# A hybrid encoder layer with grouped experts: a one-hot slot table, raw rows with factors for each slot, and bounded row transfers

## What is computed

```python
def hier_moe(a, w_group_router, b_group_router, w_expert_router, b_expert_router, w_gate, w_up, w_down):
    # a is RMSNorm(h) * g_ffn_norm; 4 groups of 8 experts, 32 in all
    gp = softmax(x @ w_group_router + b_group_router)
    g_val, g_idx = lax.top_k(gp, 1)
    el = (x @ w_expert_router + b_expert_router).reshape(T, N_GROUPS, EXPERTS_PER_GROUP)
    ep = softmax(el of the chosen group)
    e_val, e_idx = lax.top_k(ep, TOP_K)          # two experts a token
    gate = g_val * e_val / sum(e_val)
    for e in range(N_EXPERTS):
        hdn = silu(x @ w_gate[e]) * (x @ w_up[e])   # 1024 -> 256
        y = y + combine[:, e:e + 1] * (hdn @ w_down[e])   # 256 -> 1024
```

## Time and profile before

| | us |
|---|---|
| median of 3 runs | 645.04 (644.75 to 645.97) |
| the profiled execution | 643.67 |
| its span in the trace | 642.0 |
| PE busy | 530.8 (83%) |
| DVE busy | 223.6 (35%) |
| ACT busy | 147.0 (23%) |
| POOL busy | 133.2 (21%) |
| mean granted clock of PE | 0.947 of full |

### The profile page before, as it was taken

One profiled execution on the slowest core, in us unless ns is written; L12 is line 12 of the kernel. 1 busy time (PEld: TensorE's weight loads), 2 busy tenths in 40 slices (PEclk: granted clock), 3 DMA queues, 4 the chain that ended last, 5 costly groups with the idle time before them and its releaser, 6 DMA issues.

```text
span 642.0 us, 8839 instructions
## 1 busy us (share of the span) xinstructions
PE 530.8 (83%) x3092; PEld 373.3 (58%) x3093; DVE 223.6 (35%) x602; ACT 147.0 (23%) x310; POOL 133.2 (21%) x200
## 2 busy tenths in 40 slices
PE   5889999997898989999725877989788897777762
PEld 4768988884444568888624545555445564434430
DVE  4743335225959562566650211121211211111110
ACT  6734343322546221121201101010100100000000
POOL 0122232032244000034323102111201232011110
PEclk9999999999999999999856989799989999889997
DMA  8730100000620039243467999999999999999992
GB/s 333 240 142 35 32 2 1 1 0 1 236 72 27 2 137 387 100 132 133 171 227 253 405 374 388 392 367 379 388 393 390 392 392 379 403 390 392 388 363 34
DMA packets 31163, 148.81 MB, mean 232 GB/s; under 512 B 7139, under 2 KB 7798, under 8 KB 18822
## 3 DMA queue, kind: packets, MB, share of 16 engines
q1 hardware_dynamic: 25376, 128.60, 50.2%
q0 software_dynamic: 5712, 19.72, 11.7%
q10 hardware_dynamic: 38, 0.01, 0.0%
HBM read 132.48 MB, written 17.00 MB: 233 GB/s over the span
## 4 chain that ended last, share of the span: by engine, by line
DMA 45%; PE 25%; issue 10%; DVE 6%; POOL 4%; ACT 1%; POOLq 0%; SPq 0%
DMA expert_w<-in_w_down 25%; DMA expert_w<-in_w_up 19%; PE ps L476 4%; PE ps L477 4%; PE ps L481 4%; PE ps L641 3%; POOL slot_tokens L1390 2%; PE ps L582 2%; DVE p_sb L1130 2%; PE ps L596 2%; PE ps L599 1%; PE ps L628 1%; PE ps L516 1%; DMA g_rows<-token_rows,idx_now 1%; PE ps L667 1%
## 5 line engine op out<-in xcount | busy, mean ns | idle before, releaser
L767 PE MATMUL ps<-expert_w,xT 128*64 128x256 f32 x1152 | 132.2, 386 | 16.4 <-DMA expert_w<-in_w_up 6.8
L767 PEld LDWEIGHTS ps<-expert_w,xT 128*64 128x64 f32 x1152 | 97.7, 140 | 55.5 <-issue 27.8
L783 PE MATMUL ps<-expert_w,hT 128*64 128x512 f32 x288 | 76.8, 681 | 23.7 <-DMA expert_w<-in_w_down 13.2
L1432 POOL DMA_INDIRECT out<-y_sb,idx_now x18 | 28.7, 1593 | 202.6 <-DVE y_sb L1302 201.8
L783 PEld LDWEIGHTS ps<-expert_w,hT 128*64 128x64 f32 x288 | 25.5, 155 | 63.1 <-issue 60.7
L1290 DVE SCALAR_TENSOR_TENSOR hid<-s_act,gate,ps 128x256 f32<-128x256 f32 x18 | 11.9, 660 | 141.5 <-ACT s_act L968 141.5
L476 PE MATMUL ps<-w_in_hi,aT_hi 128*128 128x384 f32 (+2 forms) x120 | 43.7, 368 | 0.0
L1302 DVE COPY y_sb<-ps 128x512 f32<-128x512 f32 x18 | 12.5, 692 | 89.5 <-PE ps L783 89.5
L477 PE MATMUL ps<-w_in_lo,aT_hi 128*128 128x384 f32 (+2 forms) x120 | 40.8, 344 | 0.0
L968 ACT ACTIVATE s_act<-ps 128x256 f32<-128x256 f32 x18 | 6.9, 384 | 133.7 <-PE ps L767 133.7
L973 ACT ACTIVATE y_sb<-ps 128x512 f32<-128x512 f32 x18 | 10.8, 597 | 105.6 <-PE ps L783 105.6
(11 more groups left out here) (205 smaller groups left out, 856.5 us busy)
## 6 DMA issues: line engine op xcount, KB each, us to landing
expert_w<-in_w_gate SPq DMA_DIRECT2D x32, 1024.0 KB, 9.7
expert_w<-in_w_up SPq DMA_DIRECT2D x32, 1024.0 KB, 8.5
expert_w<-in_w_down SPq DMA_DIRECT2D x32, 1024.0 KB, 10.4
w_in_raw<-in_w_in SPq DMA_DIRECT2D x8, 608.0 KB, 10.3
w_out_raw<-in_w_out SPq DMA_DIRECT2D x8, 512.0 KB, 3.6
token_rows<-rows SPq DMA_DIRECT2D x6, 528.0 KB, 3.4
out<-h_sb SPq DMA_DIRECT2D x6, 512.0 KB, 2.9
x_sb<-in_x_prompt SPq DMA_DIRECT2D x4, 512.0 KB, 9.9
```

The lines of the kernel that those rows point to most:

```text
L767: mm = pe.matmul(ps[r, 2, g * FH:(g + 1) * FH], xT[:, q.o, k, r], w_gu(b, lane, k, g), start=(k == 0), stop=(k == KD - 1))
L783: mm = pe.matmul(ps[r, 4 + half, :], hT[:, q.o, k, r], w_dn(b, lane, k, half), start=(k == 0), stop=(k == 1))
L1432: pool.indirect_dma_start(out=out, out_offset=bass.IndirectOffsetOnAxis(ap=idx, axis=0), in_=y_sb[:, buf, :], in_offset=None, compute_op=A ...
```

## The change

The slots of a pair's first pass no longer go through DRAM. For each of a token's two experts DVE makes a row of 128 with a one at its slot (`slot_a`), ACT makes three rows of 32 with a value at its expert (`slot_b`): the token number less 768, the gate and 1/rms. PE multiplies the two and sums over all tiles (`slots`), which leaves in one bank, for each slot and expert, the token, the gate and 1/rms, zeros where there is none. The spare number is added, and that is `idx_all` and `gate_all`. The scatters stay for the second passes, and POOL itself reads their indices back.

Rows are stored and gathered as h, raw (4,096 bytes, from h_sb, issued by ACT). 1/rms goes into silu's scale and into the gate; g_ffn_norm goes into the router's weights once and into the copies of the transposed rows. The column permutation is now in the transposes, which read every eighth column. Gates of second passes come from a small table of their own by a second gather. All gathers and adds have a bound: an index over 767 moves nothing.

The small setup loads and the DRAM setup move from SP's queue to the head of POOL's, the router's weights with another layout. Pairs 1 and 2 are loaded in one go behind the last h. The out stage works in halves, with transposes, logits and routing in another order.

The diff, cut; of the loops that are wholly rewritten (PE's and DVE's over the tiles, and `slot_of`) only the new and kept lines stand:

```diff
-            small = [
-                (rope_tab[:, :, :, :].rearrange("p n t r -> p (n t r)"), a["rope"]),
-                (tok_ids[:, :], a["tokens"]),
-                (w_router[:, :, 0:EG], a["w_group_router"][0].rearrange("(p k) n -> p k n", k=KD)),
-                (w_router[:, :, EG:], a["w_expert_router"][0].rearrange("(p k) n -> p k n", k=KD)),
-            ]
+            small = [(rope_tab[:, :, :, :].rearrange("p n t r -> p (n t r)"), a["rope"])]
...
-            sp.dma_start(slot_table.rearrange("(a b) c -> a (b c)", a=P),
-                         a["slots"].rearrange("(a b) c -> a (b c)", a=P)).then_inc(setup_dram, 16)
-            sp.dma_start(table[T:T + P, :], a["zeros"]).then_inc(setup_dram, 16)
-            sp.dma_start(out[T:T + P, :], a["zeros"][:, 0:D]).then_inc(setup_dram, 16)
...
-            def store_rows(i):
-                sp.wait_ge(gates_done, i + 1)
-                sp.dma_start(table[i * P:(i + 1) * P, :], rows[:, i % 2, :]).then_inc(rows_stored, 16)
-
             for i in range(NT):
                 sp.wait_ge(h_done, 2 * (i + 1))
                 sp.dma_start(out[i * P:(i + 1) * P, :], h_sb[:, i % 2, :]).then_inc(h_stored, 16)
                 if i + 1 < NT:
                     sp.dma_start(x_res[:, :], x_dram(i + 1)).then_inc(x_res_in, 16)
-                else:
-                    load_pair(sp, 1, 1, range(3))
-                if i >= 1:
-                    store_rows(i - 1)
-            load_pair(sp, 1, 1, range(3, 4))
-            store_rows(NT - 1)
-            sp.wait_ge(slots_stored, 2 * NT * 16)
+            load_pair(sp, 1, 1)
+            load_pair(sp, 2, 2)
             sp.wait_ge(counts_done, 1)
-            sp.dma_start(idx_all[:, 0:PAIRS], slot_table[0:BLOCK, :].rearrange("(s j) c -> s (j c)", j=PAIRS)).then_inc(idx_in, 16)
-            sp.dma_start(idx_more[:, :], slot_table[BLOCK:2 * BLOCK, :].rearrange("(s j) c -> s (j c)", j=PAIRS)).then_inc(idx_rest_in, 16)
-            with nc.allow_non_contiguous_dma(reason="128 indices"):
-                sp.dma_start(idx_all[:, PAIRS:], a["slots"][0:BLOCK, :].rearrange("(s j) c -> s (j c)", j=PAIRS)[:, 0:1]).then_inc(idx_rest_in, 16)
-
-            sp.wait_ge(main.gathered[0], 16)
-            load_pair(sp, 1, 1, range(4, 6))
-            load_pair(sp, 2, 2)
...
+            def slots(i):
+
+                pe.wait_ge(slot_a_done, i + 1)
+                pe.wait_ge(slot_b_done, 3 * (i + 1))
+                for c in range(2):
+                    mm = pe.matmul(ps[:, 5, 0:3 * E], slot_a[:, c, :], slot_b[:, c, :, :].rearrange("t n e -> t (n e)"), start=(i == 0 and c == 0),
+                                   stop=(i == NT - 1 and c == 1))
+                mm.then_inc(slot_mm, 1)
...
+                out_part(i, 0, False)
+                if i >= 1:
+                    h_transposes(i - 1, 1)
+                out_part(i, 0, True)
+                if i >= 1:
+                    logits(i - 1, 0)
+                    logits(i - 1, 1)
                 if i >= 2:
+                    slots(i - 2)
+                out_part(i, 1, False)
+                h_transposes(i, 0)
+                out_part(i, 1, True)
+                if i >= 1:
+                    ranks(i - 1)
+            logits(NT - 1, 0)
+            h_transposes(NT - 1, 1)
+            logits(NT - 1, 1)
+            slots(NT - 2)
             ranks(NT - 1)
+            slots(NT - 1)
...
+                blocks = src.rearrange("t (p k) -> t k p", k=KD)
                 for k in range(KD):
-                    mm = pe.transpose(ps[:, banks + k // 4, (k % 4) * P:(k % 4 + 1) * P], src[:, k * P:(k + 1) * P], ident)
+                    mm = pe.transpose(ps[:, banks + k // 4, (k % 4) * P:(k % 4 + 1) * P], blocks[:, k, :], ident)
...
+            def slot_part(i, n, col):
+
+                for c in range(2):
+                    ins = act.activation(slot_b[:, c, n, :], route_f[:, 224 + E * c:224 + E * (c + 1)], ACT.Copy,
+                                         scale=route_f[:, col(c):col(c) + 1])
+                ins.then_inc(slot_b_done, 1)
...
                 act.wait_ge(q.x_tr, n + 1)
                 bank = 0 if q is main else 6
-                act.activation(xT[:, q.o, 0:4, :], ps[:, bank, :].rearrange("p (k t) -> p k t", k=4), ACT.Copy).then_inc(q.x_act, 1)
-
-            def silu(q, n):
+                for k in range(4):
+                    ins = act.activation(xT[:, q.o, k, :], ps[:, bank, k * P:(k + 1) * P], ACT.Copy, scale=g_x[:, k:k + 1])
+                ins.then_inc(q.x_act, 1)
+
+            def silu(q, n, g):
                 act.wait_ge(q.gu_mm, n + 1)
-                act.activation(s_act[:, q.o, :], ps[:, 2, 0:FH], ACT.Silu).then_inc(q.silu_done, 1)
+                act.wait_ge(q.gate_done, (n + 1) if q is main else 3 * (n + 1))
...
-            def second_norm(i):
...
-                dve.scalar_tensor_tensor(out=rows[:, i % 2, 0:D].rearrange("t (k p) -> t p k", k=KD),
-                                         in0=h_sb[:, i % 2, :].rearrange("t (p k) -> t p k", k=KD), scalar=route_f[:, 402:403],
-                                         in1=g_ffn[:, :].rearrange("t (p k) -> t p k", k=KD), op0=ALU.mult, op1=ALU.mult).then_inc(a2_done, 1)
...
+            def slot_of(i):
                 dve.wait_ge(rank_mm, i + 1)
                 dve.wait_ge(mask_done, i + 1)
+                rank = ps[:, 6, 0:E]
+                for c in range(2):
+                    ins = dve.tensor_tensor_reduce(out=RF[:, 320 + E * c:320 + E * (c + 1)], in0=RF[:, 224 + E * c:224 + E * (c + 1)],
+                                                   in1=rank, scale=1.0, scalar=0.0, op0=ALU.mult, op1=ALU.add,
+                                                   accum_out=RF[:, 390 + c:391 + c])
+                step(ins)
+                step(dve.tensor_scalar(RF[:, 392:394], RF[:, 390:392], float(LANE), 1024.0, ALU.is_ge, ALU.mult))
+                step(dve.scalar_tensor_tensor(out=RF[:, 394:396], in0=RF[:, 390:392], scalar=RF[:, 188:189], in1=RF[:, 392:394],
+                                              op0=ALU.add, op1=ALU.add))
+                dve.tensor_scalar(RF[:, 396:398], RF[:, 394:396], -1.0, consts[:, C_TOK + i:C_TOK + i + 1],
+                                  ALU.mult, ALU.add).then_inc(val_done, 1)
+                if i >= 1:
+                    dve.wait_ge(slot_mm, i)
+                dve.tensor_scalar(slot_a[:, 0, :], iota_slot, RF[:, 394:395], None, ALU.is_equal)
+                dve.tensor_scalar(slot_a[:, 1, :], iota_slot, RF[:, 395:396], None, ALU.is_equal).then_inc(slot_a_done, 1)
...
+                residual(i, 0)
                 if i >= 1:
                     route(i - 1)
                     route_weights(i - 1)
+                residual(i, 1)
+                if i >= 1:
+                    slot_of(i - 1)
+                    table_place(i - 1)
+                    gate_row(i - 1)
...
+            dve.wait_ge(slot_mm, NT)
+            for lane in range(2):
+                r = slice(lane * LANE, (lane + 1) * LANE)
+                dve.tensor_scalar(idx_all[r, 0:PAIRS], ps[r, 5, PAIRS * lane:PAIRS * (lane + 1)], spare_row[r], None,
+                                  ALU.add).then_inc(idx_done, 1)
+            dve.tensor_copy(idx_all[:, PAIRS:], spare_row).then_inc(idx_done, 1)
+            for lane in range(2):
+                r = slice(lane * LANE, (lane + 1) * LANE)
+                dve.tensor_copy(gate_all[r, :, :].rearrange("t j n -> t n j"),
+                                ps[r, 5, E:3 * E].rearrange("t (n e) -> t n e", n=2)[:, :, PAIRS * lane:PAIRS * (lane + 1)]).then_inc(idx_done, 1)
+            gate_row(NT - 1)
...
-                dve.tensor_copy(xT[:, q.o, 4:8, :], ps[:, bank, :].rearrange("p (k t) -> p k t", k=4)).then_inc(q.x_dve, 1)
-
-            def gates(q, src, j, n, g):
+                dve.tensor_tensor(xT[:, q.o, 4:8, :], ps[:, bank, :].rearrange("p (k t) -> p k t", k=4),
+                                  g_x[:, 4:8].unsqueeze(2).to_broadcast([P, 4, P]), ALU.mult).then_inc(q.x_dve, 1)
+
+            def gates(j, g):
+
+                dve.tensor_copy(gate[:, g:g + 1, :], gate_all[:, bass.ds(j, 1), :]).then_inc(main.gate_done, 1)
+
+            def more_gates(j):
 
                 for lane in range(2):
                     r = slice(lane * LANE, (lane + 1) * LANE)
-                    dve.tensor_copy(gate[r, g:g + 1], src[r, bass.ds(j + D + PAIRS * lane, 1)]).then_inc(q.gate_done, 1)
+                    dve.tensor_copy(gate[r, 3, 0:1], more_gate[r, bass.ds(j + PAIRS * lane, 1)]).then_inc(over.gate_done, 1)
...
+            with nc.allow_non_contiguous_dma(reason="short rows"):
+                for dst, src in ((tok_ids[:, :], a["tokens"]),
+                                 (w_router[:, :, 0:EG], a["w_group_router"][0].rearrange("(k p) n -> p k n", k=KD)),
+                                 (w_router[:, :, EG:], a["w_expert_router"][0].rearrange("(k p) n -> p k n", k=KD)),
```

(54 more changed lines are left out.)

326 lines of the change are left out of this document (182 added, 144 removed).

## The result

| | before | after |
|---|---|---|
| median of the runs, us | 645.02 (644.75 to 645.97, 4 runs) | 651.0 (650.28 to 653.41, 4 runs) |
| ratio to before | | 1.0083 (95% interval 1.0051 to 1.0115) |
| the profiled execution, us (span) | 643.67 (642.0) | 650.28 (648.5) |
| mean granted clock of PE | 0.947 | 0.939 |

The prediction was 623.0, range 613 to 638, with 9% for slower. It was wrong: the kernel did not become some 3% faster but a little slower, and the interval of the ratio lies wholly above 1.

The account below looks back on a forecast made before the run. Behind 343 us DMA work was taken as the bound, with PE waiting for weights. T0 -3.6, parts in flight -1.8, rows -21 and front +1.0 gave -25.4, the build -19.7; taking -22 gave 623 us, range 613 to 638.

Parts of the forecast that it names:

- T0: SP's first weight issue for pair 3, forecast at 366.5 us, with 78 weight parts still to be issued.
- (b): DMA work behind T0: skipping empty rows of gathers and adds saves 21 us.
- The build: Sum built up from T0 at 366.5, a start of 2 and 237 us of DMA work: last part at 605.5.
- rival 2: Bound on gathers and adds saves nothing, as skipped rows still go out or take as long: about 643 us, 7%.
- unit prices: DMA costs behind 400 us: 2.51 us a weight part, 2.15 us a row transfer, a third more per byte.
- By difference, -21: Empty rows' share of the sum of differences: 21 us saved of 25.4 in all.
- (a): Stretch up to pair 3's first issue: T0 comes at 366.5, 3.6 us earlier.
- Rival 3: Second pass's rows late (T0 + 6) or the front at its upper end (+6): 632 us, 11%.
- Parts in flight, -1.8: Weights at T0: loading one and a half parts early, less the start of an empty queue, saves 1.8 us.
- Front, +1.0: Start of the kernel: setup moved from SP's to POOL's queue costs 1.0 us, between -2.7 and +6.
- rival 1: Transposes taking every eighth element load slower and PE passes the old end: 653 us at four times, 8%.
- PE below the DMA work: Whole stretch behind T0: PE ends at 592, DMA at about 604 plus 3.7, so PE has 15 us to spare.

Follow-up runs that it names:

- spread: Changed kernel with the slots of each lane of 64 in another partition order, so empty slots no longer sit side by side: 636.4 us, ratio 0.984 to before.
- after_nobound: Changed kernel without the bounds on gathers and adds, with spare rows of zeros written to both tables: 654.3 us.
- xres2: Changed kernel with two buffers for x, so that each tile's x is loaded a tile earlier: 646.6 us.
- Combined: Changed kernel with spread slots, two buffers for x, late setup transfers and weights held until the second pass's index landed: 621.6 us, ratio 0.964 to before.

## Why the prediction was wrong, step by step

- **What bounds the kernel, 78 parts behind T0**: right. 11,232 weight packets (78 times 144) follow T0 in the changed kernel, in spread and in after_nobound, and every edit that moved T0 or the rate moved the end.
- **Work behind T0, (b)**: the step that failed most, 11.5 us. The build gave 239 us, spread took 240.1 and the changed kernel 250.5. Rows were counted over all engines (a third empty) and the saving taken from the sum of the work. As work it was there: the row packets went from 61.6 us (after_nobound) to 41.8, 19.8 less where 21 was forecast. As time 5.3 came. The engines don't share the work: by the map above the fullest moves 124 of 128 rows, 3% less, where the mean is 25% less. q0's share came out as forecast and said nothing, for it is a mean over 16 engines. The prediction's rival 2 gave "takes as long" as its condition and the adds' unchanged landing as its sign; the sign was there (10.4), but it tells little, since in spread, where the bound pays, an add lands in 10.0. The prediction gave the bound either all or nothing, never a part of its worth by place.
- **A misreading in the unit prices**: a row transfer is not a third dearer per byte than weights. 58.1 us for 15.46 MB are 3.76 us a MB, against 2.39 for weights, more than half again. And the 15.46 MB are some 29 transfers, not 27, so the price was nearer 2.0 than 2.15; that puts the forecast saving 1 to 2 us too high.
- **By difference, -21**: too much even when spread evenly, where 15.7 was measured; the build's 237 plus a start of 2 came within 1.1 us of spread's 240.1. Taking the middle of the two sums put the forecast 2.3 lower than the build.
- **T0, (a)**: forecast 366.5, measured 377.0 without the front's shift (379.76 less 2.8). Last residual to landed first gather took 21.6 us, forecast 21.5 (gather issued 12.0 later, 9.6 to land): right. The other two pieces failed. The out stage grew by 5.9 and not 2.0; xres2 puts 1.4 of that on x, the rest is open. The second pass's rows were late by 3.93 and not by 1.1, and what wasn't priced is that PE's granted clock falls in that wait (0.50 from 366 to 370): products and transposes took 9.80 and 1.97 us in place of 7.13 and 1.16. The transfers themselves cost about what was said (9 to 11 each; 11.26, 5.24 and 7.10 measured). Rival 3 is this mechanism; at T0 + 6 it was mis-sized and at 11% too rare.
- **Parts in flight, -1.8**: not there. With a part and a half in flight at T0 the kernel before took 256.1 us from there, after_nobound with none 255.8. The engines were idle for 10 us ahead of T0, and holding the early pairs back brought 8 us.
- **Front, +1.0** (-2.7 to +6): +2.8 in the profile, +1.6 as the mean of eight traces (243.0 against 241.4). In size about right. What it hid is that the head of the program was the wrong place: a gain of 3.9 was to be had, and the transfers there cost 6.7 against their late place (244.22 less 237.55), 5.4 by the mean, where the cost was put at 3.9. The other fear of that paragraph, 25 us of POOL's time to write the short rows, didn't come: the seven issues took POOL from 1.46 to 6.56 us.
- **Strided stationary operand (rival 1)**: rightly held unlikely, and excluded by the trace. Loads of the block transposes, changed kernel and before:

```profile
L761 PEld LDWEIGHTS ps<-consts_sb,g_rows 128*128 128x128 f32 x128 | 16.1, 196 | 18.0 <-DMA g_rows<-token_rows,idx_all 11.3 <-issue 5.4 <-DMA g_rows<-token_rows,idx_now 1.3
```
```profile
L754 PEld LDWEIGHTS ps<-consts_sb,g_rows 128*128 128x128 f32 x128 | 14.4, 146 | 21.3 <-DMA g_rows<-token_rows,idx_now 16.3 <-issue 5.0
```

  196 ns where it was 146, 0.4 us for eight, far from the 2.0 at which it decides.
- **PE below the DMA work**: right. Combined has a weight stream that ends at 601.4, earlier than any other, and the last part is still what PE waits for. That this is near the 604 forecast is chance, for it took four more edits.
- **Tail unchanged at 15.8**: it is 18.3. The last down products took 5.37 us in place of 3.67, at a mean granted clock of 0.71 where it was 1.00: 1.7 of the 2.5. Over the twelve traces the tail lies between 15.8 and 19.1.

## What to carry to other kernels

A saving in transfers is worth mostly what it takes from the fullest DMA engine, so ask on which partitions the skipped rows lie before you count them; a queue's mean share can't tell. Where a wait is only about 1 us off the critical path on paper, price what happens when it comes late, PE's lower clock behind it included. And weights that are loaded early are only worth something if the engines would otherwise be short of work later; ahead of a short chain of small dependent transfers they cost.

## What the runs showed of the hardware

- An index over the bound leaves packets of 4 to 8 bytes, 9 ns each in the median, where an accumulating row of 4,096 bytes takes 327 ns and a gathered one 159 (changed kernel). So a skipped row's own packets cost next to nothing.
- In indirect transfers the runs fit engines that serve partitions in groups of four, 32 apart (636.4 and 649.7 us for two orders of the same slots, 651.0 for the plain one).
- Uneven loads go with slow packets of the other queue: the median weight packet stays at 309 ns, while 264 of 9,984 took over 500 ns, against 99 with even loads and 26 and 32 without a bound.
- Seven setup transfers at the head, issued by POOL within 5 us, made w_uq 4.0 us later (27.13 against 23.16).
- One wait of PE of 3.93 us was followed by a granted clock of 0.50, and 64 products that take 7.13 us at full clock took 9.80; after a wait of 0.99 us they took 7.13.
